# FFN of a streaming encoder layer: VectorE adds the first down result of a group ahead of the remainder of the group's last gated tile

## The reference, cut to what matters

```
hn = rms_norm(h, g_pre_ffn)
f = (jax.nn.silu(hn @ w_gate) * (hn @ w_up)) @ w_down
h = h + rms_norm(f, g_post_ffn)
```

## Time and profile before

| | |
|---|---|
| median of 3 runs | 2183.42 us (2182.18 to 2185.94) |
| the profiled execution's own time | 2184.99 us |
| its span, first to last instruction | 2183.2 us |
| TensorE matmul busy | 1994.8 us, 91% |
| VectorE busy | 862.0 us, 39% |
| ScalarE busy | 514.2 us, 24% |
| GpSimd busy | 624.3 us, 29% |
| mean granted TensorE clock | 0.945 of full speed |

### The profile page before, as it was taken

How to read it: one execution, slowest core, us unless ns; L and a number is a source line. 1 busy time by engine, 2 the same in 40 slices (tenths; PEclk the granted TensorE clock), 3 DMA queues, 4 the chain that set the end, 5 groups by cost and what they waited for, 6 DMA issues and landing times.

```text
span 2183.2 us, 29969 instructions
## 1 busy us (share of the span) xinstructions
PE 1994.8 (91%) x12267; PEld 1862.6 (85%) x12267; DVE 862.0 (39%) x1618; ACT 514.2 (24%) x1248; POOL 624.3 (29%) x300
## 2 busy tenths in 40 slices
PE   6999999877688779899898989999999999999997
PEld 6999899867477679899787989988998998899895
DVE  5355206685776542620432163133223223312327
ACT  5200112264466441421331142100100000010012
POOL 4633464231000013133001313324314323341433
PEclk9999999996778779999898999999999999999998
DMA  5322241101400421211434121111101101110122
GB/s 196 122 84 99 80 139 42 65 30 40 144 1 1 169 106 49 78 55 52 156 153 164 40 78 58 47 41 39 57 20 58 38 27 50 38 48 29 48 105 107
DMA packets 55972, 161.24 MB, mean 74 GB/s; under 512 B 4160, under 2 KB 17984, under 8 KB 54464
## 3 DMA queue, kind: packets, MB, share of 16 engines
q1 hardware_dynamic: 33280, 115.04, 14.6%
q10 hardware_dynamic: 22592, 44.81, 5.9%
HBM read 131.67 MB, written 28.16 MB: 73 GB/s over the span
## 4 chain that ended last, share of the span: by engine, by line
PE 66%; DVE 11%; issue 11%; ACT 5%; POOL 3%; DMA 3%; SPq 0%; POOLq 0%; DVEq 0%; ACTq 0%
PE bank L226 19%; PE bank L230 18%; PE bank L229 18%; POOL w_hi L512 2%; DMA w_raw<-in_wall 2%; PE bank L936 1%; POOL w_lo L514 1%; DVE at_sm L1639 1%; PE bank L947 1%; PE bank L906 1%; DVE H L327 1%; DVE ACC L1873 1%; DMA H<-scratch_h 1%; DVE hid_l L1858 1%; PE bank L826 1%
## 5 line engine op out<-in xcount | busy, mean ns | idle before, releaser
L512 POOL TENSOR_TENSOR w_hi<-w_raw,one 128x1024 fp32r<-128x1024 f32 x130 | 253.2, 1947 | 1427.9 <-PE bank L226 1288.2
L226 PE MATMUL bank<-OH,w_hi 128*128 128x384 f32 x1056 | 358.5, 340 | 0.0
L229 PE MATMUL bank<-OL,w_hi 128*128 128x384 f32 x1056 | 358.3, 339 | 0.0
L230 PE MATMUL bank<-OH,w_lo 128*128 128x384 f32 x1056 | 358.1, 339 | 0.0
L514 POOL TENSOR_TENSOR w_lo<-w_raw,w_hi 128x1024 fp32r<-128x1024 f32 x130 | 325.1, 2501 | 10.2
L230 PE MATMUL bank<-w_hi,NL 128*128 128x256 f32 x864 | 245.8, 285 | 0.0
L1856 DVE TENSOR_TENSOR hr<-sg,bank 128x384 f32<-128x384 f32 x66 | 36.6, 554 | 438.1 <-PE bank L230 437.1
L229 PEld LDWEIGHTS bank<-OL,w_hi 128*128 128x128 f32 x1056 | 198.6, 188 | 0.4
L226 PEld LDWEIGHTS bank<-OH,w_hi 128*128 128x128 f32 x1056 | 198.5, 188 | 0.4
L230 PEld LDWEIGHTS bank<-OH,w_lo 128*128 128x128 f32 x1056 | 198.7, 188 | 0.0
L226 PE MATMUL bank<-w_hi,NH 128*128 128x256 f32 x576 | 165.3, 287 | 10.3 <-POOL w_lo L514 10.3
(11 more groups left out here) (327 smaller groups left out, 3912.0 us busy)
## 6 DMA issues: line engine op xcount, KB each, us to landing
w_raw<-in_wall SPq DMA_DIRECT2D x130, 512.0 KB, 3.2
scratch_h<-H ACTq DMA_DIRECT2D x6, 1536.0 KB, 5.4
cK<-in_cmk SPq DMA_DIRECT2D x8, 1024.0 KB, 6.8
cV<-in_cmv SPq DMA_DIRECT2D x8, 1024.0 KB, 4.8
H<-in_x SPq DMA_DIRECT2D x1, 4608.0 KB, 14.4
H<-scratch_h SPq DMA_DIRECT2D x1, 4608.0 KB, 18.0
Hback<-scratch_h ACTq DMA_DIRECT2D x1, 4608.0 KB, 14.1
out_y<-Hback SPq DMA_DIRECT2D x9, 512.0 KB, 2.6
```

The costliest lines, as they stand in the source:

```text
L226: m = mm(out, ah, bh, start=(i == 0), stop=False)
L229: mm(out, ah, bl, start=False, stop=False)
L230: m = mm(out, al, bh, start=False, stop=(i == n - 1))
L512: pool.tensor_tensor(whi[s][:], raw[s % 2][:], bc(one[:, 0:1], [P, WI]), ALU.mult).then_inc(w_hi, 1)
```

## The change: what moves in VectorE's order

`hidden(gi)`, which ran the six gated tiles of a group to their ends, is cut into two functions, the product (`hid_raw`) and the remainder (`hid_low`). For the last tile of a group, n = 6 gi + 5, the first `add_down` of the group before now stands between the two. The other 17 additions follow behind the remainder as they did. No instruction, no wait and no semaphore is added or removed.

```
-            def hidden(gi):
-                for n in range(6 * gi, 6 * gi + 6):
...
+            def hid_raw(n):
+                dve.wait_ge(f_sg, n + 1)
+                dve.wait_ge(f_up, 2 * n + 2)
+                if n >= 2:
+                    dve.wait_ge(f_hh, n - 1)
+                TT(g(f"hr{n % 2}")[:], g(f"sg{n % 2}")[:], B[2 * (n % 3) + 1][:, 0:NC], ALU.mult).then_inc(f_hr, 1)
+
+            def hid_low(n):
+                gi, c, f = n // 6, n % 6 // 2, n % 2
+                dve.wait_ge(f_hh, n + 1)
+                TT(g(f"hid_l{gi % 2}{f}")[:, cs(c)], g(f"hr{n % 2}")[:],
+                   g(f"hid_h{gi % 2}{f}")[:, cs(c)].bitcast(F32), ALU.subtract).then_inc(f_hl, 1)
...
-            hidden(0)
-            for gi in range(1, NG):
-                hidden(gi)
-                for q in range(2 * NT):
-                    add_down(gi - 1, q, B[6 + q % 2])
+            for gi in range(NG):
+                for n in range(6 * gi, 6 * gi + 5):
+                    hid_raw(n)
+                    hid_low(n)
+                hid_raw(6 * gi + 5)
+                if gi:
+                    add_down(gi - 1, 0, B[6])
+                hid_low(6 * gi + 5)
+                if gi:
+                    for q in range(1, 2 * NT):
+                        add_down(gi - 1, q, B[6 + q % 2])
```

## The result

The changed kernel takes 2170.21 us (median of 6 runs, 2167.70 to 2174.19), the kernel before in the same session 2184.49 us (6 runs, 2181.93 to 2186.64). The ratio is 0.9939 with a 95% interval of 0.9926 to 0.9953: 0.61% less time, 10 to 16 us. The medians differ by 14.3 us. The forecast was 11.3 us and 2172.1 us.

The account below looks back on a forecast made before the run. TensorE was taken to bound the FFN, busy 76.43 of 77.30 us per group. Ten boundary losses, 9 x 1.13 + 1.12 = 11.3 us, off the 2183.42 us median gave 2172.1 us, range 2169.5 to 2177.0.

Parts of the forecast that it names:

- What a boundary loses: TensorE loses 1.13 us at nine group boundaries and 1.12 at the first, idle plus restart, 11.3 us in all.
- The time: Whole kernel: median 2183.42 us before, less 11.3, gives 2172.1 us, 0.52% less.
- Addition 0 in its new place: Down unit 0's addition starts at 1498.98, takes 0.69 us inside w_hi without being held, leaving unit 2 0.24 us.
- The remainder is covered: Asked for at about 1499.6 within w_hi, hid_l still ends at 1500.56; the addition's 0.69 us fit its former waiting.
- What is late next: Addition 1, behind hid_l, starts at 1500.48; unit 3 keeps 0.14 us of room, enough if hid_l ends no later.
- rival 1: At the boundaries unit 3 waits for addition 1: 1.2 us over ten, 2173.3 us, or about 2176; chance 0.09.
- Rival 2: At the boundary hid_l falls behind w_lo, delaying addition 1: 1.5 us net loss, 15 in ten, 2198 us; chance 0.06.
- The rest of the way to the end: Everything after the boundaries shifts earlier with TensorE: GpSimd had 20.77 us idle, the last gain row 11.9 us to spare.
- rival 3: The ten waits vanish but TensorE waits as long for weights or at the end: 2183.4 us, no change; chance 0.05.

## Why the prediction was right, step by step

- *What a boundary loses*: 1.13 us, 11.3 in all. Measured 11.28 in the stretch, and half of it with half the boundaries. That the first matmul after a wait costs more than its idle time was needed for it: the list of waits alone gives 8.7.
- *The time*: 2170.21 us lies 1.9 below the forecast, with 14.3 us between the medians instead of 11.3. The stretch carries the forecast; the other 3 us were not in the sum, and no run shows where they come from.
- *Addition 0 in its new place*: start 0.44 us after the last matmul of unit 0 (0.43 worked out), 0.69 us long inside w_hi, and 0.24 us of room for unit 2's load (1495.25 - 1495.01), as worked out. The addition, with one operand in PSUM, is not held by GpSimd's split: the row at 1494.28 is the same pair as the one in the earlier trace rows.
- *The remainder is covered*: it ends 0.42 us behind w_hi as before (0.41), and is 0.98 us long (about 1.0).
- *What is late next*: the room for unit 3 is 1496.65 - 1496.51 = 0.14 us, the number that was worked out, and it was enough; rival 1 did not come.
- *Rival 2*, the remainder in w_lo, did not come with one addition ahead, but it is real: it came with two. Here the arithmetic of the prediction was off, in rivals 1 and 2 alike. I added 0.11 us of restart to the lateness of the weight load. The rows of before already say otherwise: the load was wanted at 1499.95 and came at 1501.21, 1.26 late, and 1.13 were lost. With two additions 0.92 late lost 0.79. In both cases a load that was late by L cost L - 0.13 us: a load in step is issued one matmul (0.23) ahead of its use, so the matmul is late by L - 0.23 only, and 0.11 of restart comes on top. The prediction left the 0.23 out. It also gave rival 2 a w_lo of 2.58 us, which is what w_lo takes when a remainder is still running at its start; in the run with two additions w_lo was ahead and took 2.40. Rival 2 is therefore dearer than the kernel before by 2.52 - 0.18 - 0.13 - 1.13 = 1.08 a boundary by this reckoning, some 11 us and not 15. Rival 1's load, 0.01 late, would cost nothing: one that was 0.05 late cost nothing (last section). That part of the rivals fell; the sum for the forecast came from the differences of the rows and did not use it.
- *The rest of the way to the end*: all of the 11.3 us arrived in the span, so rival 3 is out.

The rule of the Trainium skill ("SBUF — State Buffer", section "SBUF: two separate sides"), one port pair that the first to start holds for its whole instruction, agrees with these traces in who is held: the remainder takes 1.79 us when it meets w_hi, 2.05 when it meets w_lo, 0.55 or 0.56 with neither, and additions take 0.67 to 0.69 in any place. In the amount it does not: a remainder that was fully blocked would end its own 0.56 us behind GpSimd's instruction, and it ended 0.40 to 0.43 behind.

## What to carry to other kernels

A short wait that comes back at every pass is worth looking for in the list of waits, and its price is the difference of start times across it, not the idle column. Ask of the instruction that is late what it stands behind and whether anyone needs that one soon; if not, let it pass. When an instruction takes three times its median at some places only, look at what GpSimd does there, and at whether anyone waits for it: the remainder of a group's fifth tile is held by a w_hi too (1.41 us at 1490.30 before, 1.42 at 1485.60 after), and since the next product is not ready for another 5.9 us, that costs nothing. Moving either the addition or the split was worth the same here, and moving the remainder to a wrong place (behind two additions) gave two thirds of the gain back.

## What the runs showed of the hardware that was not expected

- A weight load that was 0.05 us late cost nothing. With the old order and GpSimd waiting, unit 2's load came at 1499.72 while the matmul ahead of it had begun at 1499.67, and the matmuls kept their step of 0.23:

```profile
1499.67 0.39 PE L230 MATMUL bank<-w_hi,hid_l 128*128 128x512 f32 x1
1499.72 0.19 PEld L226 LDWEIGHTS bank<-w_hi,hid_h 128*128 128x128 f32 x1
1499.90 0.39 PE L226 MATMUL bank<-w_hi,hid_h 128*128 128x512 f32 x1
...
1500.13 0.39 PE L229 MATMUL bank<-w_lo,hid_h 128*128 128x512 f32 x1
```

- The hold goes both ways: where GpSimd waited for down unit 0, w_hi began within the remainder at all ten boundaries and took 2.06 or 2.07 us instead of 1.89 or 1.90; w_lo took 2.57 to 2.60 instead of 2.38 to 2.41 where it began while a remainder was still running. That is less than the time they had in common: w_hi lost 0.18 us of the 0.32 (1498.75 to 1499.07).
- A remainder that was held ended 0.40 to 0.43 us behind GpSimd's instruction, in all 169 cases of the nine traces, less than its own 0.56: a part of its time seems to pass during the hold. Which part, no run here tells.
